# Hybrid decoder layer: the front's first modulation block in quarters, the norm of x on four columns, and a new order inside each block

## The reference, cut to what matters

```python
c_act = jax.nn.silu(c)
mod = c_act @ w_mod[l] + b_mod[l]                  # (2048) @ (2048 x 12288): six vectors of 2048
shift1, scale1, gate1, shift2, scale2, gate2 = split(mod, 6)
h = rms_norm(x, g_pre_mix) * (1.0 + scale1) + shift1
proj = h @ w_in[l]                                 # q, k, v, q_idx, k_idx, w_idx, pool_in, lru_in, lru_gate
bias = rel_bias[t5_bucket(pos_q - pos_k)]          # (query, key, head)
```

## Time and profile before

| | us |
|---|---|
| median of three runs | 2360.98 (2357.98 to 2363.0) |
| the profiled execution, its own time | 2359.82 |
| its span | 2358.0 |
| TensorE busy | 2286.2 (97%) |
| VectorE busy | 1438.3 (61%) |
| ScalarE busy | 897.4 (38%) |
| GpSimd busy | 574.8 (24%) |

### The profile page before, as it was taken

The page is one execution under the profiler, slowest core; times in us unless marked ns, Lnnn a source line. Parts: engine busy times, 40 slices in busy tenths (PEclk is TensorE's granted clock), DMA queues, the critical chain, the costliest instruction groups (busy, mean ns, idle before and its releaser), DMA issues.

```text
span 2358.0 us, 33974 instructions
## 1 busy us (share of the span) xinstructions
PE 2286.2 (97%) x13060; PEld 1926.9 (82%) x13060; DVE 1438.3 (61%) x1788; ACT 897.4 (38%) x1187; POOL 574.8 (24%) x344
## 2 busy tenths in 40 slices
PE   5989999999989999989999999999999999999998
PEld 1558787888767788889999999999888888888886
DVE  6648984893138574898777777776544333333335
ACT  4333424322337322755444444444222223222222
POOL 6544454444437000000000000002999200000000
PEclk8999999999999999999999999999999999999999
DMA  8886655333333376333333333335776445444443
GB/s 312 344 303 222 247 202 162 97 93 97 90 102 95 131 288 223 116 126 135 134 133 133 133 133 133 133 133 190 240 221 214 155 141 197 143 137 145 135 125 138
DMA packets 129760, 391.21 MB, mean 166 GB/s; under 512 B 18320, under 2 KB 19984, under 8 KB 117520
## 3 DMA queue, kind: packets, MB, share of 16 engines
q1 hardware_dynamic: 115408, 347.65, 43.1%
q10 hardware_dynamic: 9664, 25.70, 2.8%
q0 software_dynamic: 4608, 16.78, 2.4%
HBM read 356.25 MB, written 33.57 MB: 165 GB/s over the span
## 4 chain that ended last, share of the span: by engine, by line
PE 56%; DVE 1%; ACT 0%; issue 0%; DVEq 0%; ACTq 0%; PEldq 0%
PE psum L904 19%; PE psum L905 19%; PE psum L906 19%; DVE B_raw L2356 0%; DVE T_lo L2340 0%; PE psum L1331 0%; DVE w_lo L2251 0%; ACT T_hi L1711 0%; ACT sq_end L1368 0%; DVE x_in L2489 0%; DVE B_lo L2340 0%; DVE unit_odd L2270 0%; DVE unit_odd L2273 0%; DVEq L231 0%; DVE y L2471 0%
## 5 line engine op out<-in xcount | busy, mean ns | idle before, releaser
L2278 DVE TENSOR_TENSOR w_lo<-raw,w_hi 128x1024 fp32r<-128x1024 f32 x128 | 176.1, 1376 | 424.0 <-ACT w_hi L1657 424.0
L904 PE MATMUL psum<-w_hi,uin_hi 128*128 128x512 f32 x1024 | 407.3, 398 | 0.0
L905 PE MATMUL psum<-w_lo,uin_hi 128*128 128x512 f32 x1024 | 405.8, 396 | 0.0
L906 PE MATMUL psum<-w_hi,uin_lo 128*128 128x512 f32 x1024 | 403.5, 394 | 0.0
L822 POOL TENSOR_TENSOR w_lo<-raw,w_hi 128x1024 fp32r<-128x1024 f32 (+1 forms) x96 | 254.6, 2657 | 348.7 <-ACT w_hi L1361 348.7
L1657 ACT ACTIVATE w_hi<-raw 128x1024 fp32r<-128x1024 f32 x128 | 135.8, 1061 | 489.6 <-PE psum L906 475.2
L904 PE MATMUL psum<-T_hi,w_hi 128*128 128x256 f32 x1024 | 288.2, 281 | 5.4 <-DVE w_lo L2251 5.4
L906 PE MATMUL psum<-T_hi,w_lo 128*128 128x256 f32 x1024 | 287.9, 281 | 0.0
L905 PE MATMUL psum<-T_lo,w_hi 128*128 128x256 f32 x1024 | 287.9, 281 | 0.0
L1361 ACT ACTIVATE w_hi<-raw 128x1024 fp32r<-128x1024 f32 (+1 forms) x128 | 128.7, 1013 | 327.9 <-PE psum L906 295.7
L904 PE MATMUL psum<-h_hi,w_hi 128*128 128x512 f32 (+1 forms) x592 | 237.8, 402 | 6.7 <-issue 4.0
(11 more groups left out here) (329 smaller groups left out, 4447.2 us busy)
## 6 DMA issues: line engine op xcount, KB each, us to landing
raw<-in_w_mlp_down SPq DMA_DIRECT2D x128, 512.0 KB, 3.9
raw<-in_w_in SPq DMA_DIRECT2D x88, 512.0 KB, 3.8
mod_ring<-in_w_mod_first SPq DMA_DIRECT2D x32, 1024.0 KB, 8.9
mod_slab<-in_w_mod SPq DMA_DIRECT2D x32, 1024.0 KB, 5.3
raw<-in_w_up_units SPq DMA_DIRECT2D x64, 512.0 KB, 4.4
unit_odd<-in_w_up_units SPq DMA_DIRECT2D x64, 512.0 KB, 5.0
uin<-u_s SPq DMA_DIRECT2D x128, 256.0 KB, 4.2
raw<-in_w_out SPq DMA_DIRECT2D x32, 512.0 KB, 5.8
```

The lines of the kernel that those rows point to most:

```text
L904: nc.tensor.matmul(o, a_hi, b_hi, start=first, stop=False)
L905: nc.tensor.matmul(o, a_hi, b_lo, start=False, stop=False)
L906: return nc.tensor.matmul(o, a_lo, b_hi, start=False, stop=last)
L2278: V.tensor_tensor(w_lo[:, slot, :, :], raw[:, slot, :, :], w_hi[:, slot, :, :].bitcast(F32), ALU.subtract).then_inc(down_lo, 1)
```

## The change

It does four things. (1) The mod rows of the first block are four calls (`mod_rows_of(b, q)`) laid between the banks 4 to 7 and the norm of x. (2) The norm's sum over partitions gives four columns (tokens on partitions) instead of a row on all partitions; VectorE's `rsqrt` works on 128 x 4; four transposes of the broadcast column bring it back to a row, and ScalarE copies it to x_rstd. (3) SP issues the ring quarters of block b+1 behind the slabs of block b, that is ahead of the slabs of block b+1. (4) Inside a block TensorE runs the rows of b+1 between the banks and the slabs of b, and the columns of b+1 behind them; VectorE, ScalarE and GpSimd have new orders to match.

```diff
--- before.py
+++ after.py
@@ tiles, semaphores
-        pick = at(57, "pick", [P, P], F32)
+        pick = at(57, "pick", [P, 1], F32)
...
@@ -616,11 +615,14 @@
             sp.dma_start(col[:], columns_in).then_inc(cols_in, 16)
             for t in range(TT):
                 sp.dma_start(x_t[:, 4 * t:4 * t + 4, :], x_turned[:, 4 * t:4 * t + 4, :]).then_inc(x_landed[t], 16)
+            for q in range(4):
+                load_ring(q)
             for b in range(MOD_BLOCKS):
-                for q in range(4):
-                    load_ring(4 * b + q)
                 load_slab(2 * b)
                 load_slab(2 * b + 1)
+                if b + 1 < MOD_BLOCKS:
+                    for q in range(4):
+                        load_ring(4 * (b + 1) + q)
             def load_bias(it):
 
                 sp.dma_start(bm_of(it), bias_h[it // TT][:, it % TT, :]).then_inc(bias_landed[it % BM_SLOTS], 16)
@@ -826,10 +828,11 @@
             for i in range(BIAS_FIRST):
                 bias_steps(i)
             for b in range(MOD_BLOCKS):
-                for i in range(BIAS_BLOCK):
-                    bias_steps(BIAS_FIRST + BIAS_BLOCK * b + i)
+                bias_steps(BIAS_FIRST + BIAS_BLOCK * b)
                 low(2 * b)
                 low(2 * b + 1)
+                for i in range(1, BIAS_BLOCK):
+                    bias_steps(BIAS_FIRST + BIAS_BLOCK * b + i)
             for s in range(2 * SG, PROJ_SLABS):
                 low(s)
@@ mod_rows_of(b, q): the loop over q is gone, its body unchanged
-            def mod_rows_of(b):
-
-                for q in range(4):
...
+            def mod_rows_of(b, q):
+
+                g = 4 * b + q
...
@@ first_slab(s): one slab instead of a loop over both
-            def first_slabs(b):
...
+            def first_slab(s):
...
@@ -1019,20 +1022,41 @@
             last.then_inc(xsum_done, 1)
             pe.wait_ge(consts, 1)
             pe.wait_ge(xrows_ready, 1)
-            nc.tensor.matmul(psum[:, XALL_BANK, :], pick[:], x_rows[:], start=True, stop=True).then_inc(xall_done, 1)
-            for i in range(TT, BIAS_FIRST):
-                bias_bank(i)
+            for t in range(TT):
+                last = nc.tensor.matmul(psum[:, XALL_BANK, t:t + 1], x_rows[:, P * t:P * t + P], pick[:], start=True, stop=True)
+            last.then_inc(xcols_done, 1)
+            bias_bank(4)
             pe.wait_ge(c_ready, 1)
+            mod_rows_of(0, 0)
+            pe.wait_ge(rstd_ready, 1)
+            pe.wait_ge(ident_ready, 1)
+            for t in range(TT):
+                last = nc.tensor.transpose(psum[:, XSUM_BANK, P * t:P * t + P], stat[:, 2, t:t + 1].to_broadcast([P, P]), ident[:])
+            last.then_inc(xall_done, 1)
+            mod_rows_of(0, 1)
+            bias_bank(5)
+            mod_rows_of(0, 2)
+            bias_bank(6)
+            mod_rows_of(0, 3)
+            bias_bank(7)
+            mod_columns_of(0)
             for b in range(MOD_BLOCKS):
                 i = BIAS_FIRST + BIAS_BLOCK * b
-                mod_rows_of(b)
+                more = b + 1 < MOD_BLOCKS
                 bias_bank(i)
+                if more:
+                    mod_rows_of(b + 1, 0)
                 bias_bank(i + 1)
-                mod_columns_of(b)
+                if more:
+                    mod_rows_of(b + 1, 1)
+                first_slab(2 * b)
+                if more:
+                    mod_rows_of(b + 1, 2)
+                    mod_rows_of(b + 1, 3)
+                first_slab(2 * b + 1)
+                if more:
+                    mod_columns_of(b + 1)
                 bias_bank(i + 2)
-                if b >= 1:
-                    first_slabs(b - 1)
-            first_slabs(MOD_BLOCKS - 1)
 
             h = (h_hi, h_lo)
@@ -1400,30 +1424,44 @@
                 for k in range(4 * q, 4 * q + 4):
                     nc.scalar.activation(x_sq[:, k, :], x_t[:, k, :], ACT.Square).then_inc(xsq_ready, 1)
                 bias_store(q)
-            act.wait_ge(xsum_done, 1)
-            nc.scalar.activation(x_rows[:], psum[:, XSUM_BANK, :], ACT.Copy).then_inc(xrows_ready, 1)
-            act.wait_ge(consts, 1)
-            act.wait_ge(xall_done, 1)
-            nc.scalar.activation(x_root[:], psum[:, XALL_BANK, :], ACT.Sqrt, bias=eps_c[:], scale=1.0 / D).then_inc(root_ready, 1)
-            for i in range(TT, BIAS_FIRST):
-                bias_store(i)
-            split(0)
-            split(1)
-            for b in range(MOD_BLOCKS):
-                i = BIAS_FIRST + BIAS_BLOCK * b
+            def mod_rows_copy(b):
                 act.wait_ge(ring_used, 4 * b + 4)
                 if b >= 1:
                     act.wait_ge(cols_done, b)
                 nc.scalar.activation(mod_rows[:], psum[:, MOD_BANK, :], ACT.Copy).then_inc(rows_copied, 1)
-                bias_store(i)
-                bias_store(i + 1)
+
+            def h_block(b):
                 act.wait_ge(mul_ready, b + 1)
                 act.wait_ge(xn_ready, KS * b + KS)
                 h_high(0, 2 * b, x_t[:, 2 * b, :], h_hi)
                 h_high(0, 2 * b + 1, x_t[:, 2 * b + 1, :], h_hi)
-                bias_store(i + 2)
+
+            act.wait_ge(xsum_done, 1)
+            nc.scalar.activation(x_rows[:], psum[:, XSUM_BANK, :], ACT.Copy).then_inc(xrows_ready, 1)
+            act.wait_ge(consts, 2)
+            act.wait_ge(xcols_done, 1)
+            nc.scalar.activation(stat[:, 1, 0:TT], psum[:, XALL_BANK, 0:TT], ACT.Sqrt, bias=eps_c[:],
+                                 scale=1.0 / D).then_inc(root_ready, 1)
+            bias_store(4)
+            act.wait_ge(xall_done, 1)
+            nc.scalar.activation(x_rstd[:], psum[:, XSUM_BANK, :], ACT.Copy).then_inc(xrstd_ready, 1)
+            bias_store(5)
+            bias_store(6)
+            mod_rows_copy(0)
+            bias_store(7)
+            split(0)
+            split(1)
+            h_block(0)
+            for b in range(MOD_BLOCKS):
+                i = BIAS_FIRST + BIAS_BLOCK * b
+                bias_store(i)
+                bias_store(i + 1)
                 split(2 * b + 2)
                 split(2 * b + 3)
+                if b + 1 < MOD_BLOCKS:
+                    mod_rows_copy(b + 1)
+                    h_block(b + 1)
+                bias_store(i + 2)
             act.wait_ge(consts, 2)
             s = 2 * SG + 2
@@ -1894,13 +1932,10 @@
 
             def x_norm():
 
+                dve.wait_ge(consts, 2)
                 dve.wait_ge(root_ready, 1)
-                ch.put(V.tensor_scalar(x_var[:], psum[:, XALL_BANK, :], 1.0 / D, EPS, ALU.mult, ALU.add))
-                ch.link(V.reciprocal(x_rstd[:], x_root[:]))
-                ch.link(V.tensor_tensor(x_root[:], x_rstd[:], x_rstd[:], ALU.mult))
-                ch.link(V.tensor_tensor(x_root[:], x_root[:], x_var[:], ALU.mult))
-                ch.link(V.tensor_scalar(x_root[:], x_root[:], -0.5, 1.5, ALU.mult, ALU.add))
-                ch.link(V.tensor_tensor(x_rstd[:], x_rstd[:], x_root[:], ALU.mult))
+                rsqrt(psum[:, XALL_BANK, 0:TT], TT, stat[:, 2, 0:TT], 1.0 / D, stat[:, 2, 8:8 + TT])
+                dve.sem_inc(rstd_ready, 1)
 
             def x_scaled(k):
@@ -1965,19 +2000,36 @@
                                         ALU.mult, ALU.add))
                 V.tensor_tensor(lo[:, k, :], h_full[:, k % 2, :], hi[:, k, :].bitcast(F32), ALU.subtract).then_inc(h_ready, 1)
 
-            for i in range(BIAS_FIRST):
-                bias_steps(i)
-            x_norm()
-            for b in range(MOD_BLOCKS):
-                for i in range(BIAS_BLOCK):
-                    bias_steps(BIAS_FIRST + BIAS_BLOCK * b + i)
-                x_scaled(2 * b)
-                x_scaled(2 * b + 1)
-                mod_columns(b)
+            def h_block(b):
+
                 dve.wait_ge(xn_ready, KS * b + KS)
                 for k in (2 * b, 2 * b + 1):
                     dve.wait_ge(h_hi_ready, k + 1)
                     h_low(0, k, x_t[:, k, :], h_hi, h_lo)
+
+            for i in range(5):
+                bias_steps(i)
+            bias_steps(5)
+            x_norm()
+            bias_steps(6)
+            dve.wait_ge(xrstd_ready, 1)
+            x_scaled(0)
+            x_scaled(1)
+            bias_steps(7)
+            bias_steps(8)
+            mod_columns(0)
+            h_block(0)
+            for b in range(MOD_BLOCKS):
+                i = BIAS_FIRST + BIAS_BLOCK * b
+                bias_steps(i + 1)
+                if b + 1 < MOD_BLOCKS:
+                    x_scaled(2 * b + 2)
+                    x_scaled(2 * b + 3)
+                bias_steps(i + 2)
+                if b + 1 < MOD_BLOCKS:
+                    bias_steps(i + 3)
+                    mod_columns(b + 1)
+                    h_block(b + 1)
                 if b == 2:
                     softplus()
```

More of the change, by code:

```diff
@@ L284, in build @@
         x_sq = at(20, "x_sq", [P, KD, T], F32)
-        x_var = at(0, "x_var", [P, T], F32)
-        x_root = at(2, "x_root", [P, T], F32)
```

(27 more changed lines are left out.)

## The result

Measured: 2394.2 us median (2390.0 to 2396.5, four runs) against 2362.0 in the same call, ratio 1.0133, 95% interval 1.0111 to 1.0155. The change makes the kernel slower by 1.3%. The direction was forecast; the time lies 19 us above the forecast of 2375, at the upper end of the range and about twice as far from before as I had said (32 against 15). Three executions in the second call of experiments (e5 to e8) had a granted clock of 0.65 to 0.75 and took 2833 to 3219 us; the ratios leave them out, the medians do not.

A forecast was written before the change was run, and what follows sets the result against it. TensorE was taken to bound the steady block. Second columns 62.6, six periods of 17.4, 14.7 and 5.1 put g2 at 186.8 against 174.2 (+12.6); low clock 2.6 made +15.2 on 2359.8: 2375 us, range 2360 to 2395.

The forecast's parts named there:

- six periods of 17.4: Blocks between the second and the last columns: 17.4 us each, against 15.06 before, added to 62.6 to give 167.0.
- The norm and the quarters: Start of the front: shorter norm chain with row quarters under it, first columns at 42.0, 6.7 us before 48.71.
- The wait in every block: Third bank behind the columns gets VectorE's steps only after h: 2.0 us of wait added in every block.
- The first pass: First to second columns, 42.0 to 62.6: bank waits for h and GpSimd's step, h_hi at 44.8, low clock 2 us.
- Rival 4: VectorE in seven blocks: GpSimd holds h for one step, 1.6 us each, 11 more, 2386 us; chance 0.05.
- Rival 5: Start of the front: quarter 1 waits behind the transposes, columns near 48, 2381 us; chance 0.05.
- rivals 2 and 3: Blocks: 2, start's gain kept, 2351 us, chance 0.11; 3, stall of about 0.8 us a block, 2361 us, chance 0.15.
- The low clock: TensorE's slab products after a further stall or so: clock drops, 0.43 us a product instead of 0.235, costing 2.6 us.
- rival 1: TensorE at low clock in most blocks: 7 x 2.6 us on top of 12.6, 2391 us; chance 0.20.
- The end of the front: Last columns to g2: 14.7 us, then 5.1 instead of 3.5, bank 31's copy ahead of ki_hi costing 1.6.
- The transfers: Block loads and stores: next quarters issued ahead of slabs, 14.0 us a block at 400 GB/s, staying hidden.
- rival C of e1: Loads in e1: new order starves or crowds queues, period stays over 17, 2385 to 2394 us; no chance given.

The follow-up runs named there:

- e5: Kernel after with four moves: third bank's steps earlier, softplus ahead of mod_columns, bank 7's copy behind h, bank 31's behind ki_hi; 2354.9 us, ratio 0.9974.
- e8: Kernel after, unchanged, profiled once more; one execution, span 2387.3 us.
- e1: Kernel after with VectorE making the third bank's steps one turn earlier, ahead of mod_columns and h; 2365.8 us, ratio 1.0025.
- e2: Kernel after with softplus moved from behind h of block 4 to ahead of that block's mod_columns; 2383.5 us, ratio 1.0099.
- e6: New start (norm on four columns, block 1's rows in quarters) with the block order of the kernel before on all engines; 2364.6 us, ratio 1.0006.
- e7: Kernel before, unchanged, profiled once more; one execution, 2368.9 us.
- e3: Kernel after with ScalarE's copy of bank 7 moved behind the first two splits and h_hi of block 1; 2393.5 us, ratio 1.0137.
- e4: Kernel after with ScalarE's copy of bank 31 moved behind ki_hi and the index weights; 2391.2 us, ratio 1.0122.

## Why the prediction was right and wrong, point by point

The mechanism that I had called deciding was there. Two terms of the sum failed, by some 6.5 us each: the "six periods of 17.4" left softplus out of VectorE's order and so put it at nothing, and the 20.6 of the first pass (42.0 to 62.6) was too small. Together they are 13 of the 17 us by which g2 came later than forecast.

**The norm and the quarters: right.** First columns at 42.0 forecast, 41.30 measured; transposes 1.1 forecast, 1.05 from start to start.

**The wait in every block: right.** Period 17.4 forecast, 17.57 measured where nothing else came in, and e1 shows the cause by taking it away. That this step was in the order of VectorE's program, and not in any duration, is what made it findable before the run.

**What stood behind h: one step left out.** I walked VectorE's order for the steady block and let "block" stand for all of them. Softplus, 22 operations that run once, sits at the end of the third turn. In the kernel before it fell into VectorE's idle time ahead of the columns; the new order put it between h of block 4 and the steps that TensorE was waiting for. The sum's "six periods of 17.4" was short by 6.6 us there (24.14 against 17.57): 4.4 of longer wait, the rest at the low clock. e2 takes back 6.5 of it. This is the step of the prediction that failed.

**The first pass: its term was mis-sized.** I named the chain (bank 5's store, bank 7's copy, splits, h_hi, GpSimd's step) but priced the landing so that h_hi came at 44.8; it came at 48.12, 3.3 us later. The store took 7.9 us to land (38.07 to 45.94) against 2.6 for one issued at 34.41 in the kernel before. That one met a DMA share of 0.47 on average, this one 1.01, for four ring quarters go out between 34.49 and 40.8, where before they waited till 38.39. That the loads slow the landing is argued from this, from e6 (7.99 us) and from the 8.1 us of e7, since no run moved the loads alone. Then the first h operation took 1.87 instead of 0.55: it ran until 50.93, just behind GpSimd's w_lo (48.29 to 50.64). From h_hi to the steps of VectorE were 5.5 us instead of the 3.7 of the steady block. These steps, from 53.64, released the bank, and not GpSimd's step, which I had last at 50.3 and which was ready at about 52.4 (an estimate: 50.62 and a third of the 5.40 of its three). So the bank ended at 57.1 instead of 51. First pass 27.1 instead of 20.6: 6.5 us. What hangs on the landing is shown by e3 and e5, which take bank 7's copy out of the way (22.81 and 19.27), and by e6, where the same wait eats the gain.

The prediction weighed the rule of the Trainium skill (SBUF — State Buffer, Who interferes with whom) that of a VectorE and a GpSimd instruction that contend the second is held until the first is done. The 1.87 beside w_lo agrees, and the 2.09 of e3 and e5 (0.16 without w_lo) still more clearly; the 0.92 beside GpSimd's steps in every block again shows less than a full hold. Rival 4 fell with it: h took as long in every steady block as in the kernel before, and the period was 17.57. Rival 5 fell with the first columns at 41.30, rivals 2 and 3 with the period.

**The low clock: in kind right, in size wrong.** I counted 2.6 us for one in the sum and gave 2.6 each to rival 1. The trace has the clock at 0.50 in four blocks behind the first pass:

```profile
95.00:96.00 1.00, 1.00 (x6) 0.50 0.95 369
...
116.00:117.00 1.00, 1.00 (x11) 0.50 0.00 0
...
174.00:175.00 1.00, 1.00 (x4) 0.50 0.66 260
```

(stretches of 1 us; the fourth is at 190). It costs a steady block 19.16 - 17.57 = 1.6 us, not 2.6, for it was shorter than behind the front: the clock fell within the us from 93 (mean 0.85) and was back within that from 97 (0.95). Rival 1's condition, a low clock in most of seven blocks, came true by four to three here and not in e8, where three had one. Its price did not: 1.6, 2.2 and 1.6 in the periods and 1.2 behind the last columns (20.17 against the 19.00 of e2, which had none there) are 6.6 us, not 18.2. That its 2391 lies nearer to the measured time than my 2375 is luck, since softplus and the first pass fill the difference. e1 shows that the blocks that had a low clock owed it to the wait.

**The end of the front: right, partly by luck.** From the last columns to g2 19.8 forecast, 20.2 measured. The last slab ended 0.9 later than forecast, at a low clock, and g2 followed it by 4.6 instead of 5.1 us; bank 31's copy ahead of ki_hi cost 1.2 (e4), not 1.6.

**The transfers: right, but the step on SP was none.** Ring 1, slabs, ring 2, slabs is what SP issued before as well: the loop was cut at another place, and the list of loads is the same. Point (3) of the change and the prediction describe a moved step where nothing moved, and rival C of e1 (the new order of the loads) had no new order to test. What did move is when each quarter's wait ends, and by the argument above that is what crowded bank 5's store.

**The sum.** g2 forecast at 186.8, measured at 203.8: 6.5 for the first pass, 6.6 for softplus, 3.2 for two low clocks in it, 1.0 for 0.17 in each of six periods, 0.4 in the tail, less 0.7 at the start, make 17.0. Against the forecast's 2.6 for a low clock stand the 7.1 of the MLP loop in the profiled execution. The spread that I gave the forecast, 2366 to 2386, doesn't follow from its terms: with six periods of 17.1 and no low clock the sum gives about 2371, with 17.9 and two low clocks about 2381.

## What to carry to other kernels

When engines run programs in a fixed order, write down for each wait what stands ahead of the awaited instruction on its engine in every turn, the ones with an `if` in them too; the one move that mattered here, steps made before h instead of behind it, changed no work at all and brought the end of the front 29 us forward (some 26 us of the time). A buffer that waits for its store to land depends on what else is in the queues: where loads went out earlier, a wait of 5 us appeared on an engine that had nothing to do with them. A gain at the start of a pipeline is worth what its next wait leaves of it; here 7 us were gone by the second columns, and in the start alone (e6) nothing is left of them in the time. With all four moves (e5) about 6 are.

## What the runs showed of the hardware that I had not expected

The same kernel, at a granted clock of 1.00 throughout that loop, runs the 256-column products of the MLP loop at 855, 845 or 835 starts per 100 us, in one execution or another; over the loop of some 600 us that is 7 us a step. The cause stays open: TensorE shows no idle time there, and the DMA shares are alike. A 256 KB store took 2.6 us to land when no load was in flight and 7.9 to 8.1 with 1 MB loads beside it, at a DMA share of 0.98 to 1.01. An operation of VectorE on 128x2 elements took 2.09 us instead of 0.16 beside a GpSimd subtraction on 128x1024 that had begun 0.27 us before it, and ended with it (e3).
